# A two-layer model on one core: group norm with one variance per head, mixing stages with early loads, halves of the exponentials added first

## The reference

```python
    y = rwkv7_scan(r, decay, k, v, kk, a)
    mu = jnp.mean(y, axis=-1, keepdims=True)
    var = jnp.mean(jnp.square(y - mu), axis=-1, keepdims=True)
    y = (y - mu) * lax.rsqrt(var + GN_EPS) * gn_g.astype(f32) + gn_b.astype(f32)
...
    y = jnp.concatenate([y_rwkv, y_attn], axis=-1) @ w_out
    return x + y
```

## Time and profile before

| | us |
|---|---|
| median of 3 runs (lowest, highest) | 4506.92 (4504.72, 4507.43) |
| the profiled execution, its span | 4512.46, 4510.6 |
| PE busy (weight loads beside it) | 3992.4, 89% (2784.7) |
| DVE busy | 2765.1, 61% |
| ACT busy | 2174.5, 48% |
| POOL busy | 1144.9, 25% |
| TensorE's granted clock, mean | 0.935 |

### The profile page before, as it was taken

One profiled execution on the slowest core, in us unless ns is written; L12 is line 12 of the kernel. 1 busy time (PEld: TensorE's weight loads), 2 busy tenths in 40 slices (PEclk: granted clock), 3 DMA queues, 4 the chain that ended last, 5 costly groups with the idle time before them and its releaser, 6 DMA issues. The chain is left out here.

```text
span 4510.6 us, 75715 instructions
## 1 busy us (share of the span) xinstructions
PE 3992.4 (89%) x30840; PEld 2784.7 (62%) x30840; DVE 2765.1 (61%) x5076; ACT 2174.5 (48%) x3171; POOL 1144.9 (25%) x919
## 2 busy tenths in 40 slices
PE   7999999758988888887669899797999999999879
PEld 5767767445656556655458687585555555555467
DVE  5556464557768788888565323244676777777433
ACT  4445354586788778787433323122333333333431
POOL 1111111135434343433101000000344444444100
PEclk9999999878989999898679899898999999999989
DMA  4334233311211211211056533465223232322143
GB/s 129 96 106 128 80 109 98 92 38 37 49 33 40 50 40 35 55 41 30 26 177 202 197 127 127 170 222 170 48 64 71 55 80 55 71 65 49 50 165 113
DMA packets 388091, 404.92 MB, mean 90 GB/s; under 512 B 115776, under 2 KB 287488, under 8 KB 387488
## 3 DMA queue, kind: packets, MB, share of 16 engines
q1 hardware_dynamic: 385648, 393.10, 30.3%
q10 hardware_dynamic: 2096, 6.99, 0.4%
HBM read 248.36 MB, written 151.62 MB: 89 GB/s over the span
## 5 line engine op out<-in xcount | busy, mean ns | idle before, releaser
L142 ACT ACTIVATE PT<-psum 128x1024 f32<-128x1024 f32 x384 | 394.2, 1027 | 699.0 <-PE psum L132 695.6
L170 DVE TENSOR_REDUCE m<-psum 128x1 f32<-128x1024 f32 x384 | 467.8, 1221 | 302.3 <-PE psum L132 302.3
L132 PE MATMUL psum<-xc,wah 128*128 128x512 f32 x1600 | 514.6, 403 | 3.2 <-DVE xc L146 2.9
L146 POOL TENSOR_TENSOR part<-PT 128x1024 f32<-128x1024 f32 x144 | 342.0, 2375 | 558.2 <-DVE all L146 381.9
L132 PE MATMUL psum<-PT,V 128*64 128x512 f32 x1536 | 370.3, 603 | 0.0
L143 ACT ACTIVATE bias<-score,cand,cols 128x2048 bf16<-128x2048 f32 (+6 forms) x217 | 314.4, 1449 | 100.9 <-DVE cand L158 97.2
L132 PEld LDWEIGHTS psum<-xc,wah 128*128 128x128 f32 x1600 | 299.7, 190 | 79.4 <-issue 10.3
L143 ACT ACTIVATE sgn<-score,cand,cols 128x1920 bf16<-128x1920 f32 (+6 forms) x217 | 291.1, 1342 | 118.9 <-DVE cand L158 114.4
L146 POOL TENSOR_TENSOR Lm<-gm,cst 64x512 f32<-64x512 f32 x192 | 258.9, 1348 | 302.8 <-PE psum L132 154.0
L132 PE MATMUL psum<-hc,w4h 128*128 128x512 f32 x1024 | 321.0, 395 | 11.3 <-ACT w4h L142 11.3
L132 PE MATMUL psum<-xc,wal 128*128 128x512 f32 x800 | 315.7, 395 | 0.0
(11 more groups left out here) (334 smaller groups left out, 8790.9 us busy)
## 6 DMA issues: line engine op xcount, KB each, us to landing
raw_a<-in_w_a SPq DMA_DIRECT2D x50, 512.0 KB, 4.0
raw_w<-in_w_in SPq DMA_DIRECT2D x32, 512.0 KB, 4.4
QNh<-scr_qnh SPq DMA_DIRECT2D x48, 256.0 KB, 5.2
QRh<-scr_qrh SPq DMA_DIRECT2D x96, 128.0 KB, 5.0
QNl<-scr_qnl SPq DMA_DIRECT2D x48, 256.0 KB, 6.9
xin<-in_x SPq DMA_DIRECT2D x16, 512.0 KB, 4.1
scr_AR<-AR SPq DMA_DIRECT2D x32, 256.0 KB, 2.2
scr_BK<-BK SPq DMA_DIRECT2D x32, 256.0 KB, 2.3
```

Source lines behind the costliest of these rows:

```text
L132: return self.e.matmul(out, a, b, start=start, stop=stop, skip_group_check=True)
L142: return self.e.activation(out, src, f, bias=bias, scale=scale)
L146: return self.e.tensor_tensor(out, a, b, op) if self.e else self.vector(out)
L170: return self.e.tensor_reduce(out, a, AX, op, negate=negate) if self.e else self.vector(a)
```

## The change

1. **Group norm.** `gn1` is now four matmuls of `y2` by `heads_of` (two columns of `blk`), which leave one sum per token and head; DVE scales them into `iv` (128x8), POOL raises that to the power -0.5. A new piece `gn2` spreads `iv` with eight matmuls (64x128 outputs against the identity) into bank 2, DVE multiplies `yc` by it, POOL applies gain and shift. ACT takes no square root any more.
2. **First mixing stage.** Its tile 0 is rows 512 to 639, and the rows go round (`rows_of`); stage 4 takes its chunks of 512 columns in that order. Chunks 0 to 5 of the weights, `x[0]` and `y[0]` to `y[2]` are issued by SP in stage 2, chunk 6 by SP and chunk 7 by ACT behind the barrier. Pads in SBUF keep the buffers apart from those that stage 2 still uses.
3. **Stage 5.** A piece `half` at r = 2 of each unit adds the two halves of each `all5` on DVE (two adds of 128x512); `sum` takes two matmuls instead of four.
4. **Its end.** The first pieces of `order_m` stand among the last of `order_5`; `qmt` 0 and 1 are loaded with the last `gat`; `x[0]` and all eight weight chunks of the second mixing stage are issued at `m1` 1, its first three `y` tiles at `mout` 5.

```diff
@@ group norm, pe_2 / dve_2 / pool_2 (act_2 loses its gn1)
-                        q.mm(bank[2], blk, y2[:, :, :]).then_inc(*s_pe.up("gn1", i))
+                        for h in range(4):
+                            t = q.mm(bank[2][:, 2 * h:2 * h + 2], y2[:, h, :], heads_of)
+                        t.then_inc(*s_pe.up("gn1", i))
                     else:
+                        q.wait_ge(s_pool, "iv", i)
+                        for h in range(4):
+                            for e in range(2):
+                                t = q.mm(bank[2][64 * e:64 * e + 64, 128 * h:128 * h + 128],
+                                         iv[:, 2 * h + e:2 * h + e + 1].broadcast_to([128, 64]), ident)
+                        t.then_inc(*s_pe.up("gn2", i))
...
-                    q.act(y2[:, :, :], quads(bank[2]), ACT.Sqrt, bias=epg[:, :], scale=1.0 / 64).then_inc(*s_act.up("gn", i))
...
-                    q.recip(y2[:, :, :], y2[:, :, :]).then_inc(*s_dve.up("iv", i))
+                    q.ts(iv[:, :], bank[2][:, 0:8], 1.0 / 64, 64e-5, ALU.mult, ALU.add).then_inc(*s_dve.up("gv", i))
+                elif what == "gn2":
+                    q.tt(yc[:, :, :], yc[:, :, :], quads(bank[2]), ALU.mult).then_inc(*s_dve.up("yn", i))
...
+                    q.tt(iv[:, :], iv[:, :], neghalf[:, 0:8], ALU.pow).then_inc(*s_pool.up("iv", i))
-                    q.tt(yc[:, :, :], yc[:, :, :], y2[:, :, :], ALU.mult).then_inc(*s_pool.up("yn", i))
@@ early loads, sp_2
+                    if nth(b) == 3:
+                        q.wait_ge(t_pe, "pv", b - 1, 3, last_of[b - 1])
+                        for c in range(6):
+                            q.dma(mix1.raw[c][:, :], mix1.weight[c]).then_inc(*mix1.d_w[c].up(c))
+                    if nth(b) == 1:
+                        q.wait_ge(k_act, "in", b - 2)
+                        q.wait_ge(k_act, "in", b - 1)
+                        q.wait_ge(d_yo, 6)
...
@@ class Mix
+            def rows_of(self, i):
+                n = (i + 4) % NT if self.top else i
+                return slice(128 * n, 128 * n + 128)
@@ stage 5
+            if u and r == 2:
+                order_5.append(("half", u - 1))
...
+        order_5 = order_5[:done] + order_m[:1] + end_5[:2] + order_m[1:3] + end_5[2:]
+        order_5 += order_m[3:]
...
-                    q.wait_ge(q_dve, "acc", 8 * u + 7)
-                    for x in range(2):
-                        for w in range(2):
-                            t = q.mm(bank[6 + u % 2][64 * w:64 * w + 64, :], one[:, 0:64], all5[u % 2][w][:, x, :], x == 0, x == 1)
+                    q.wait_ge(q_dve, "half", u)
+                    for w in range(2):
+                        t = q.mm(bank[6 + u % 2][64 * w:64 * w + 64, :], one[:, 0:64], all5[u % 2][w][:, 0, :])
...
+                elif what == "half":
+                    u = k[1]
+                    for w in range(2):
+                        q.wait_ge(q_dve, "acc", 8 * u + 6 + w)
+                        t = q.tt(all5[u % 2][w][:, 0, :], all5[u % 2][w][:, 0, :], all5[u % 2][w][:, 1, :], ALU.add)
+                    t.then_inc(*q_dve.up("half", u))
```

More of the change, by code:

```diff
@@ L1062, in weight @@
             return {"ld": 9.0, "gram": 2.5, "lv0": 4.0, "lvy": 1.8, "lvl": 1.2, "lvu": 1.2, "ldw": 6.0, "sm": 0.5, "sa": 1.2, "sb": 1.3,
-                    "sc": 2.0, "gn0": 3.0, "gn1": 5.0, "kT": 0.9, "vv": 0.9}.get(what, 0.4)
+                    "sc": 2.0, "gn0": 3.0, "gn1": 2.0, "gn2": 4.0, "kT": 0.9, "vv": 0.9}.get(what, 0.4)
         def inv_pieces(i):
@@ L1074, in seq_pieces @@
                 out += [("sm", i, c), ("sa", i, c)] + [("yout", i - 1) if c == 0 else ("lds", i)] + [("sb", i, c), ("sc", i, c)]
-            return [k for k in out if k != ("yout", -1)] + [("gn0", i), ("gn1", i)]
+            return [k for k in out if k != ("yout", -1)] + [("gn0", i), ("gn1", i), ("gn2", i)]
         rwkv_order = []
@@ L1171, in lane_2 @@
             return {"ld": "inverse", "gram": "inverse", "lv0": "inverse", "lvy": "inverse", "lvl": "inverse", "lvu": "inverse", "gn0": "norm",
-                    "gn1": "norm", "yout": "norm", "kT": "kv", "vv": "kv", "qd": "scores", "score": "scores", "exp": "scores", "pT": "values",
+                    "gn1": "norm", "gn2": "norm", "yout": "norm", "kT": "kv", "vv": "kv", "qd": "scores", "score": "scores", "exp": "scores", "pT": "values",
                     "pv": "values", "rb": "values", "fin": "values"}.get(what, "chunks")
@@ L1355, in pe_2 @@
                     t.then_inc(*s_pe.up("y", i, c))
-                elif what in ("gn0", "gn1"):
+                elif what in ("gn0", "gn1", "gn2"):
                     i = k[1]
@@ L1717, in pool_2 @@
                 what = k[0]
-                if what in ("gn1", "log", "nobias", "eq", "tie"):
+                if what in ("gn1", "gn2", "log", "nobias", "eq", "tie"):
                     q.wait_ge(i_pool, "lm", *halves)
@@ L1790, in program @@
         P2.c.close()
+        PAD_V, PAD_S = 1480, 512
         class Mix:
@@ L1858, in mix_sp @@
                     c = k[1]
-                    if c % 2 == 0:
+                    if c == 6 and M.top:
                         q.dma(M.raw[c][:, :], M.weight[c]).then_inc(*M.d_w[c].up(c))
@@ L1935, in mix_act @@
                 q.dma(M.g2[:, :], A["g_row2"]).then_inc(*M.d_g2.up())
-            for c in range(1, 8, 2):
-                q.dma(M.raw[c][:, :], M.weight[c]).then_inc(*M.d_w[c].up(c))
+            if M.top:
+                q.dma(M.raw[7][:, :], M.weight[7]).then_inc(*M.d_w[7].up(7))
             for k in q.pieces(M.order):
@@ L2694, in columns @@
             return slice(1024 * (u % 2) + 512 * w, 1024 * (u % 2) + 512 * w + 512)
+        mix2 = Mix("m2", "y2T", A["w_out2"], scratch["x1"], A["final_g2"], False)
+        done = order_5.index(("acc", NST - 1)) + 1
+        end_5 = order_5[done:]
+        assert [k[0] for k in end_5] == ["half", "sum"] + ["rc"] * 4 + ["out"]
+        order_5 = order_5[:done] + order_m[:1] + end_5[:2] + order_m[1:3] + end_5[2:]
+        order_5 += order_m[3:]
         def sp_5(q):
@@ L2701, in sp_5 @@
                     u = k[1]
+                    if u == NUN - 1:
+                        for m in range(2):
+                            q.dma(qmt[m][:, :], feat("qm")[:, 0, 512 * m:512 * m + 512]).then_inc(*d_qm[m].up(m))
                     h = u // 2
@@ L2726, in sp_5 @@
                               y5[u % 2][64 * w:64 * w + 64, :, :]).then_inc(*d_y5[u % 2].up(u, w))
-            for k in order_m:
-                if k[0] == "m1" and k[1] % 4 == 0:
+                elif k[0] == "m1":
+                    if k[1] == 1:
+                        q.wait_ge(q_pe, "pv", NST // 2 - 1, 1)
+                        q.dma(mix2.x[0][:, :], mix2.resid[0:128, :]).then_inc(*mix2.d_r[0].up(0))
+                        for c in range(8):
+                            q.dma(mix2.raw[c][:, :], mix2.weight[c]).then_inc(*mix2.d_w[c].up(c))
+                    if k[1] % 4:
+                        continue
                     m = k[1] // 4
@@ L2743, in sp_5 @@
                           y5[m % 2][:, :, :]).then_inc(*d_y5[m % 2].up("m", m))
+                    if m == 5:
+                        q.wait_ge(d_y5[0], "m", 4)
+                        for i in range(3):
+                            q.dma(mix2.y[i][:, :, :], feat("y2T")[:, :, 128 * i:128 * i + 128]).then_inc(*mix2.d_y[i].up(i))
             q.wait_ge(d_y5[0], "m", 6)
@@ L2882, in act_5 @@
                               scale=sc).then_inc(*q_act.up("exp", g, e))
-            for k in order_m:
-                what = k[0]
-                if what == "m1":
+                elif k[0] == "m1":
                     n = k[1]
@@ L2894, in act_5 @@
                     t.then_inc(*e_act.up("exp", n))
-                elif what == "m2":
+                elif k[0] == "m2":
                     n = k[1]
@@ L2942, in dve_5 @@
                     q.tt(y5[u % 2][:, :, :], y5[u % 2][:, :, :], rc5[:, :, :], ALU.mult).then_inc(*q_dve.up("y", u))
-            for k in order_m:
-                what = k[0]
-                if what == "m1":
+                elif what == "m1":
                     n = k[1]
```

109 lines of the change are left out of this document (68 added, 41 removed).

## The result

| | before | after |
|---|---|---|
| median of 4 runs (lowest, highest), us | 4507.18 (4504.72, 4510.25) | 4439.08 (4437.09, 4444.24) |
| the profiled execution, its span | 4512.46, 4510.6 | 4438.31, 4436.5 |
| ratio, 95% interval | | 0.985 (0.9833 to 0.9867) |

The change takes 68 us off, where 56 were forecast; 4439 against 4451, inside the range of 4402 to 4486. Of all executions reported in this document one is set aside, the slowest of the six of the last kernel: 5640.5 us at a mean granted clock of 0.728, where the other five had 0.944 to 0.947. The two spans differ by 74.1, since the profiled execution of before was some 5 above its median.

What follows compares the result with a forecast made beforehand. Limits: hand-offs between engines in stage 2, a load at the first mixing stage's head, TensorE in stage 5. -31 - 25 + 16 - 8.2 + 4.3 - 11.8 = -56; against the median 4506.92, 4451 us; range 4402 to 4486.

Steps and rivals of the forecast that it cites:

- I take a microsecond of each of the three as equally likely to be on the path: Stage 2: each microsecond of TensorE, VectorE or ScalarE counts 0.434; times (-86.3 + 14.9) gives -31 us.
- 15 us more of TensorE: Stage 2: twelve small matmuls for one of 128x512 add 0.93 us per tile, 14.9 in all.
- the head: First mixing stage: early loads and angle rows behind all wl bring the first matmul from 2299.47 to 2274.4, -25 us.
- The rest keeps its pace: First mixing stage behind its first matmul: VectorE makes one wl after another as before, so no further change.
- The tail's start: End of stage 5: memory attention's first output matmuls start at 4221.3, not 4229.47, -8.2 us.
- The queue in front of the last `qmt`: Memory attention: three y tiles, 1.5 MB, ahead on SP's queue take 5 us, of which +4.3 show.
- The last head: Second mixing stage: first matmul at 4311.7, not 4323.46, -11.8 us.
- Halves not held: Rival, stage 5: VectorE's two adds slip in before GpSimd's, or the reduce has slack; -20 for +16, 4415 us, chance 0.20.
- Stage 2 hides its part: Rival: the threshold search alone sets stage 2 and the norm lay in gaps; 4482 to 4497 us, chance 0.17.
- Stage 2 gives all: Rival: all the time saved on ScalarE and VectorE shortens stage 2, -86; 4396 us, chance 0.08.
- Late loads: Rival, first mixing stage: early loads sit behind late waits on SP's queue; -13 for -25, 4463 us, chance 0.05.
- TensorE waiting for `iv`: Slower rival, stage 2: gn2's matmuls wait for GpSimd's power, 3.7 us a tile, +59 for -31; 4541 us, chance 0.05.

Runs made afterwards that it cites:

- the last kernel: Changed kernel with halves added behind the second reduce, second mixing stage's y tiles loaded behind the last qmt and gat, yh and one yl low: 4392.5 us.
- The runs: Changed kernel with unused square roots and table loads back on ScalarE: 4470.21 us; separately, with unused reciprocals of 128x512 back on VectorE: 4451.73 us.
- The run that imitates such a chain: Changed kernel with ScalarE's root and VectorE's reciprocal put back, gn1's small scaling waiting for both: 4482.03 us, stage 2 at 1434.4.

## Why the prediction was right, and where it was wrong

**Part 3 was right, by its mechanism and by its size.** A row of the kernel before showed a VectorE add of two SBUF operands standing still until GpSimd's was through the earlier trace rows; the adds were to end at GpSimd's end and 1.1 us more, and they end 1.15 after it; TensorE was to wait 1.6 and waits 1.46; +16 was forecast for the stage, +14.8 measured, or +17.9 against the run without halves. Taking the halves away or putting them 2.4 us later undoes it.

**Part 1 was mis-sized: -31, measured -57.** The step that failed was "I take a microsecond of each of the three as equally likely to be on the path". The runs give ScalarE 0.6 and VectorE 0.1. At 0.434 each the 100 us of both, put back, would be 43; they are 33, and that this is near -31 is an accident. What the forecast had no term for is the chain: in the old norm bank 2 and the reciprocal waited for a table load and a root. The run that imitates such a chain gives 10 more, from one execution, and 11 of the old norm's cost stay open. The forecast's 15 us more of TensorE were too many as well: by the groups after, the twelve small matmuls are busy 8 x 0.069 + 4 x 0.137 = 1.10 a tile, 0.54 more than the old one. And "a power of 128x8, shorter" was false; 1.671 against 1.376. It cost nothing that shows, because at that place nothing waited for GpSimd: the `gn2` matmuls have 0.0 idle ahead of them in the groups after.

**Part 2 was right at the head (-25, -24.9) and blind behind it.** "The rest keeps its pace" failed twice: the tiles run 0.29 slower because the pads that make early loads possible pushed `yh` and `yl` up, and the transposes of one early tile wait 0.89 for VectorE, whose angle rows now lie there (read from the trace, not tried). The remaining 0.7 is stage 4's first weights, 12.06 against 11.35 after the last transposes. Nothing in the trace of before could show the first.

**Part 4 was right in kind.** The tail's start gave 6.7 of 8.2. The queue in front of the last `qmt` cost 6.7 and not 4.3: the idle went from 0.95 to 6.31, which is 5.4, and the matmuls behind that gap ran at a granted clock of 0.50, which the step left out. That 4.3 of the 5 us would show was worked out from no row. The last head gave 11.5 of 11.8.

**The rivals.** Halves not held: refuted by the 3.39. Stage 2 hides its part: refuted. Stage 2 gives all: the 57 lie halfway between the forecast's 31 and its 86, and ScalarE's part and VectorE's part were not equal shares of them. Late loads: refuted, the first matmul comes 5.07 behind the barrier and waits for no load. TensorE waiting for `iv`: the 0.0 above, and the stage is 57 shorter.

**The total was in part luck.** It lay 12 from the forecast in the medians, 18 in the traces. Stage 2 alone was 26 off, and 6 of that were covered by a cost of the first mixing stage that nobody had foreseen. Of the four parts, the third and the head of the second came as they were worked out.

## What to carry to other kernels

Before moving an add to VectorE, look where GpSimd is at that moment: the same pair of adds cost 3.4 us behind one reduce and 1.3 behind the next, and with the wait it causes that is 38 us over the program. Idle shares don't price work in a stage that three engines share; put the removed work back, off the chain and on it, and measure, more than once where the answer is of the size of the spread. And a head start for loads should go behind the last load that somebody still waits for.

## What was not expected of the hardware

The same fp32r matmuls (128x128 operand, 512 columns) step at 0.227 us with the 128x128 operands at bytes 103,808 to 120,191 of a partition and at 0.232 to 0.233 with them from 169,120 on; with one of the three there, all steps of the tile are slow. In the second mixing stage, with them at 128,384 to 144,767, the changed kernel's tiles still run at 0.227. A power of 128x8 takes GpSimd 1.67 us, longer than its multiply of 128x512 (1.376).
